# Seven-product gate and up projections in the first FFN of a two-block transformer kernel

## The chip, the cores and the metric

One core of one Trainium2 chip runs the kernel. The metric is the device time of one execution in microseconds (us); the kernel before takes 1641.35 us (median of three runs, 1639.81 to 1642.16).

## What is computed

A sequence of 512 tokens with model width 1024 goes through two transformer blocks, in fp32. Only the first block's feed-forward network (FFN) changes:

```python
h = rms_norm(x, norm_ffn_g)
x = x + (silu(h @ w_gate_ffn) * (h @ w_up_ffn)) @ w_down_ffn   # 1024 -> 2816 -> 1024
```

The second block has an FFN of the same size (with a causal convolution), which stays as it is. Every matmul is done in three passes, high x high, high x low and low x high parts of weight and activation, in fp32r.

## The kernel before, in words

**Tiles and chunks.** Activations lie transposed: 8 blocks of 128 features by 512 tokens (`X`). Weights come as chunks of 128 x 1024 fp32 (512 KB, 8 tiles of 128 x 128). PLAN (L62 to L90) lists all 336 chunks in the order of use. SyncE (SP) loads chunk i into one of five `raw` buffers (`load`, L2813); before it issues, it waits until VectorE (DVE) has split chunk i-5 (L2819). ScalarE (ACT) copies `raw` to the high part `WH` (recorded at L1132), DVE subtracts to get the low part `WL` (L1828); there are three such pairs. TensorE (PE) then runs 24 matmuls on the chunk (8 tiles x 3 passes, `mm3`, recorded at L504). PE waits for the split chunk, so a late load stops everything.

**First FFN.** Hidden width 2816 is 22 tiles of 128. Gate and up projections take one chunk for each tile and each side, 44 in all, as 24 matmuls with 512 moving columns each. DVE scales by the rms factor, ACT applies silu, DVE multiplies. The down projection already uses Winograd's form of Strassen's seven products of 2x2 blocks for most of its work (`down`, L837): pairs of hidden tiles, pairs of output tiles and two halves of 256 tokens are the blocks. `combine` (L2128) and `pair_lo` (L2141) form the sums of activations in `TH` and `TL`; each product is a run of matmuls with 256 moving columns. Two phases hold 12 and 10 hidden tiles. In the second phase only half of the outputs are made with seven products; the rest is done plainly by `last` with 512 columns over the last 10 hidden tiles (LAST, L34).

**Sums of weights.** Seven products need sums of weight blocks too. They are made in HBM during the run. SP copies a plane (one quarter of a weight matrix, 2.88 MB) to `sums` in four pieces, each followed by one chunk load (`copy_in`, L2834). GpSimd (POOL) then issues one accumulating DMA, which adds a second plane to it (`sum_in`, L2693). The third and the fourth sums start from finished ones, so SP waits on a semaphore for POOL's DMA before it copies (L2836), and POOL for SP's copies (L2694).

**What sets the order.** Each engine has its own program. SP's is a plain list (L2845 to L2902): while it waits for something, it loads no chunk. In the mixer stage the order of POOL, PE, ACT and DVE is written out by hand (`mixer_order_pool` and its likes). POOL there masks attention scores (L2687) and adds the second branch's output to `X` (L2663, the last of eight additions ends at 353 us); behind it come `sum_in(1, 0, ...)` and `sum_in(1, 1, ...)`, the eight additions of the third branch, a wait for the reload of x, and `sum_in(1, 2, ...)`.

**The stretch 300 to 450 us.** Chunks 44 to 55 are `mix2`, 56 to 67 `mix0`, 68 to 75 `w_out`, then `wk_xa` and `wv_xa`, eight each. Before `w_out`, SP waits for POOL's last addition and then reloads memT (1 MB) and x (2 MB) with L2867 and L2869; `w_out` adds its result to the reloaded x, and each output's PSUM bank (of three) is held until that add is done.

## Time and profile before

| what | value |
|---|---|
| median of three runs | 1641.35 us |
| span of the profiled execution | 1636.7 us |
| PE busy | 1621.8 us, 99% |
| DVE busy | 1010.2 us, 62% |
| ACT busy | 731.6 us, 45% |
| DMA moved | 225.96 MB, mean 138 GB/s |

The profiled execution's own time is known as its span, 1636.7 us from its first to its last instruction; the runs' median is 4.65 us above that. A busy share of PE says how long matmuls were in flight; the pitch from one matmul's start to the next says how fast they go. "Landing" of a DMA is the time from issue to its last byte. The software queue is POOL's (the accumulating DMAs), the hardware queue SP's.

### The profile page before, as it was taken

Reading aid. Unit: us, or ns where it says so; the run is one execution under the profiler, and the core shown is the slowest. Engines: PE = TensorE matmul, PEld = TensorE weight load, DVE = VectorE, ACT = ScalarE, POOL = GpSimd, SP = SyncE. Lnnn points to the kernel's source line nnn. Section 1 sums busy time; section 2 is a strip of 40 time slices with the busy share of each in tenths; the row PEclk is TensorE's granted clock in tenths of the full one; section 3 lists DMA queues with packets and bytes.
Section 4 is the critical chain, followed back from the end, with each engine's and each line's share of the span. In section 5 each row is a group of like instructions: output and inputs, shape, how many; then the busy total and the mean of one; then the engine's idle time right before and its main releaser. Section 6 shows DMA issues by size and latency. Waiting matters only on the chain.

```text
span 1636.7 us, 21111 instructions
## 1 busy us (share of the span) xinstructions
PE 1621.8 (99%) x8434; PEld 1342.7 (82%) x8434; DVE 1010.2 (62%) x1460; ACT 731.6 (45%) x1105; POOL 153.5 (9%) x172
## 2 busy tenths in 40 slices
PE   9999999999999999999999999999999999999999
PEld 7788878888878778888988887877777888898889
DVE  5346754455663454656656576757655588867886
ACT  5344334333553344334433356256685554544453
POOL 0000001221210011000000051212201200000000
DMA  7343222348754115768776443332114232363226
GB/s 258 102 183 113 91 91 65 101 128 268 227 164 141 52 65 164 223 212 217 217 241 189 126 158 116 117 129 65 65 39 131 81 104 92 114 201 109 91 89 181
DMA packets 60083, 225.96 MB, mean 138 GB/s; under 512 B 6657, under 2 KB 7041, under 8 KB 56337
## 3 DMA queue, kind: packets, MB, share of 16 engines
q1 hardware_dynamic: 55856, 197.29, 36.0%
q0 software_dynamic: 3840, 26.77, 7.6%
q8 instruction: 67, 1.10, 0.3%
q10 hardware_dynamic: 288, 0.54, 0.1%
q14 instruction: 32, 0.25, 0.0%
HBM read 220.35 MB, written 50.36 MB: 165 GB/s over the span
## 4 chain that ended last, share of the span: by engine, by line
PE 94%; DVE 2%; ACT 2%; issue 1%; DMA 0%; POOL 0%; SPq 0%; DVEq 0%; ACTq 0%; POOLq 0%
PE pst L504 93%; PE pst L1013 1%; PE pst L672 1%; DVE WL L1828 1%; ACT WH L1132 0%; DMA raw<-wst 0%; ACT L1137 0%; DVE qx L2072 0%; ACT misc L1132 0%; POOL acc L2653 0%; DVE XL L1840 0%; PE pst L794 0%; DVE ML L1836 0%; DVE misc L2607 0%; DVE X L2178 0%
## 5 line engine op out<-in xcount | busy, mean ns | idle before, releaser
L504 PE MATMUL pst<-XH,WH 128*128 128x512 f32 x1312 | 523.0, 399 | 0.6 <-DVE WL L1828 0.6
L1828 DVE TENSOR_TENSOR WL<-raw,WH 128x1024 fp32r<-128x1024 f32 (+2 forms) x334 | 381.5, 1143 | 220.1 <-ACT WH L1132 219.4
L504 PE MATMUL pst<-XH,WL 128*128 128x512 f32 x1312 | 511.6, 390 | 0.0
L504 PE MATMUL pst<-XL,WH 128*128 128x512 f32 x1312 | 511.1, 390 | 0.0
L1132 ACT ACTIVATE WH<-raw 128x1024 fp32r<-128x1024 f32 (+3 forms) x336 | 326.4, 975 | 314.5 <-PE pst L504 308.3
L504 PEld LDWEIGHTS pst<-XH,WH 128*128 128x128 f32 x1312 | 246.3, 188 | 61.4 <-issue 11.5
L504 PEld LDWEIGHTS pst<-XL,WH 128*128 128x128 f32 x1312 | 246.5, 188 | 52.0 <-issue 2.6
L504 PEld LDWEIGHTS pst<-XH,WL 128*128 128x128 f32 x1312 | 246.3, 188 | 51.9
L504 PE MATMUL pst<-TH,WH 128*128 128x256 f32 (+1 forms) x586 | 170.6, 291 | 1.6 <-DVE X L2178 1.0
L504 PE MATMUL pst<-TL,WH 128*128 128x256 f32 (+1 forms) x586 | 170.2, 290 | 0.0
L504 PE MATMUL pst<-TH,WL 128*128 128x256 f32 (+1 forms) x586 | 170.1, 290 | 0.0
L1132 ACT ACTIVATE misc<-misc 128x512 f32<-128x512 f32 x86 | 54.3, 631 | 148.8 <-DVE misc L2239 80.7
L504 PEld LDWEIGHTS pst<-TH,WH 128*128 128x128 f32 x586 | 112.3, 192 | 4.2 <-issue 1.7
L504 PEld LDWEIGHTS pst<-TL,WH 128*128 128x128 f32 x586 | 112.3, 192 | 1.7
L504 PEld LDWEIGHTS pst<-TH,WL 128*128 128x128 f32 x586 | 112.3, 192 | 1.6
L504 PE MATMUL pst<-ZH,WH 128*128 128x512 f32 x224 | 89.2, 398 | 0.0
L504 PE MATMUL pst<-ZH,WL 128*128 128x512 f32 x224 | 87.3, 390 | 0.0
L504 PE MATMUL pst<-ZL,WH 128*128 128x512 f32 x224 | 87.3, 390 | 0.0
L2653 POOL TENSOR_TENSOR acc<-acc,misc 128x512 f32<-128x512 f32 x35 | 59.3, 1695 | 280.5 <-ACT misc L1132 279.2
L2607 DVE SCALAR_TENSOR_TENSOR misc<-gp,colsb,misc 128x512 f32<-128x512 f32 x88 | 66.1, 751 | 23.4 <-ACT misc L1132 21.8
L1132 ACT ACTIVATE TH<-misc 128x512 fp32r<-128x512 f32 (+1 forms) x88 | 50.8, 586 | 45.0 <-DVE misc L2614 31.6
L1132 ACT ACTIVATE misc<-gp,colsb 128x512 f32<-128x512 f32 x44 | 35.9, 815 | 58.2 <-DVE gp L2633 58.2
(286 smaller groups left out, 1905.0 us busy)
## 6 DMA issues: line engine op xcount, KB each, us to landing
raw<-wst SPq DMA_DIRECT2D x237, 512.0 KB, 3.4
sums<-wd POOLq DMA_DIRECT2D x8, 2816.0 KB, 19.8
raw<-sums SPq DMA_DIRECT2D x32, 384.0 KB, 3.2
sums<-wd SPq DMA_DIRECT2D x16, 704.0 KB, 5.8
sums<-sums SPq DMA_DIRECT2D x16, 704.0 KB, 6.0
raw<-wd SPq DMA_DIRECT2D x24, 384.0 KB, 3.1
raw<-sums SPq DMA_DIRECT2D x24, 320.0 KB, 3.0
raw<-wd SPq DMA_DIRECT2D x18, 320.0 KB, 3.1
```

The costliest lines, as they stand in the source:

```text
L504: return nc.tensor.matmul(out, lhs, rhs, start=start, stop=stop, skip_group_check=more)
L672: ins = nc.tensor.transpose(ps[b0 + e][:, j * P:(j + 1) * P], sg_[:, s, e, j * P:(j + 1) * P], ident)
L1013: ins = nc.tensor.transpose(ps[b0 + e][:, j * P:(j + 1) * P], Sx[:, s, e, j * P:(j + 1) * P], ident)
L1132: return nc.scalar.activation(out, in_, func, **kw)
L1828: vec.tensor_tensor(WL[:, i % NHL, 0:n], raw[:, i % NRAW, 0:n], WH[:, i % NHL, 0:n].bitcast(F32), ALU.subtract).then_inc(wl, 1)
L2607: vec.scalar_tensor_tensor(o, gp[:, e, j:T + j], col[:, a:a + 1], o, ALU.mult, ALU.add).then_inc(hs, 1)
L2653: gp.tensor_tensor(acc[:, which, :], acc[:, which, :], sq[j % 2], ALU.add).then_inc(acp, 1)
```

## The change

1. The gate and up projections become seven products for each hidden tile: the 2x2 blocks are (even, odd input tiles) x (gate, up) for weights and (even, odd input tiles) x (token halves) for activations. Each product is 4 x 3 matmuls of 256 columns. 154 products go in pairs into 77 chunks of 1024, in a hand-made order (`up_order`).
2. Partial results are carried in PSUM: ACT copies product p1 into the bank where p2 accumulates, and p6 into the bank where p5 and p3 follow; two SBUF copies go to `acc`. In the second and third phase a matmul on `ones_r` primes the banks of the first two tiles.
3. The sums of the normed input are made once by `gained` (ACT and DVE), during `wo_xa`.
4. The hidden tiles go in three phases of 8, 8 and 6. The down projection's chunks hold two products. `last` covers 6 hidden tiles.
5. Sums of the gate and up weights are new (plane 5.77 MB; 8 copy pieces and 2 accumulating DMAs each); all copies and sums get new places in SP's and POOL's programs.

The diff, cut to its core:

```diff
-LAST = 10
+LAST = 6
-PAIRS = ((0, 6), (6, 5))
+PAIRS = {1: ((0, 4), (4, 4), (8, 3)), 2: ((0, 6), (6, 5))}
+DOWN_SEQ = {1: (MP_SEQ, MP_SEQ, MP_SEQ[:14]), 2: (MP_SEQ, MP_SEQ)}
+UP_N = HID * 4 * P * P
+PIECES = (2, 1, 1)
+def up_order(ph):
+    a, z = TILES[1][ph][0], TILES[1][ph][-1]
...
+    for m in range(a + 2, z + 1):
+        order += [(m, "p6"), (m - 1, "p3"), (m, "p7"), (m, "p2"), (m, "p5")]
+        order += [(m + 1, "p1")] if m < z else []
+        order += [(m - 1, "p4")]
+    return order + [(z, "p3"), (z, "p4")]
...
+            def ups1(ph):                                  (PE)
+                first = TILES[1][ph][0]
+                for x, (m, prod) in enumerate(UP_SEQ[ph]):
+                    if x % 2 == 0:
+                        h, l = (units(w) for w in chunk("ffn_up1"))
...
+                    if prod == "p1":
+                        if ph and m < first + 2:
+                            free(m % 2)
+                            mm(ps[m % 2][:, :], ones_r[:, :], XCH[:, 0:T]).then_inc(u_prime.sem, 1)
+                        free(4 + m % 2)
...
+                    elif prod in ("p2", "p6"):
+                        pe.wait_ge(u_seed, m + 1)
+                        if prod == "p2" and UP_AT[m, "p6"] < UP_AT[m, "p2"]:
+                            pe.wait_ge(u_seed2, m + 1)
...
+                    for k in range(4):
...
+                        ins = mm3(up_bank(m, prod), h[:, w, :], l[:, w, :], XCH[:, t], XCL[:, t], not more and k == 0, k == 3, more)
...
+                    if prod == "p1":                       (ACT)
...
+                        run(ACT.Copy, up_bank(m, "p2"), up_bank(m, "p1")).then_inc(u_seed.sem, 1)
+                    elif prod == "p6":
+                        run(ACT.Copy, up_bank(m, "p5"), up_bank(m, "p6")).then_inc(u_seed2.sem, 1)
...
+                        run(ACT.Copy, acc[:, m % 2, 0:256], up_bank(m, "p6")).then_inc(u_s.sem, 1)
+                    elif prod == "p5":
+                        run(ACT.Copy, acc[:, m % 2, 256:T], up_bank(m, "p5")).then_inc(u_y.sem, 1)
...
+                def half_b(m):                             (DVE)
...
+                    vec.tensor_tensor(U, up_bank(m, "p7"), U, ALU.subtract).then_inc(u_b.sem, 1)
+                def half_a(m):
...
+                    vec.tensor_tensor(U, up_bank(m, "p4"), U, ALU.subtract).then_inc(u_a.sem, 1)
...
+            def sum_in(w, to, plane, ready):               (POOL)
+                rows_ = [a.rearrange("(r c) -> r c", c=2048) for a in (sums[w][to], parts[w][plane])]
+                pool.wait_ge(d_copy if w else xs_out, ready)
+                for x in range(PIECES[w]):
+                    gp.dma_start(rows_[0][352 * x:352 * x + 352], rows_[1][352 * x:352 * x + 352], accum_op=ALU.add, max_dma_last_dim=8192).then_inc(d_sum if w else eg_in, 16)
...
+                    if x == 22:
+                        sum_in(0, 0, 3, 256)
+                        sum_in(0, 1, 3, 256)
...
             follow(mixer_order_pool, {"main": twice(mixer()), ...
+            sum_in(0, 2, 0, 384)
             sum_in(1, 0, 3, 128)
             sum_in(1, 1, 3, 128)
             drain(branch(2))
+            sum_in(0, 3, 1, 512)
             pool.wait_ge(x_in[3], 32)
+            for k in range(7):
+                add_squares()
             sum_in(1, 2, 0, 192)
+            sum_in(1, 3, 1, 256)
...
+            def copy_in(w, to, src, ready=None, pace=1):   (SP)
+                if ready:
+                    sp.wait_ge(d_sum if w else eg_in, ready)
...
+                for x in range(4 * PIECES[w]):
+                    nc.sync.dma_start(rows_[0][176 * x:176 * x + 176], rows_[1][176 * x:176 * x + 176]).then_inc(d_copy if w else xs_out, 16)
+                    load(pace)
...
-            load_to("zu", 0, 5)
-            copy_in(1, 0, wd[0][2])
-            copy_in(1, 1, wd[0][0])
-            load_to("mix0", 9, 5)
-            copy_in(1, 2, sums[0][0], 32)
+            load_to("q", 2, 5)
+            copy_in(0, 0, wup[2])
+            copy_in(0, 1, wup[0])
+            load_to("mix1", 5, 5)
+            copy_in(0, 2, sums[0][0], 64)
+            copy_in(1, 0, wd1[2])
+            copy_in(1, 1, wd1[0])
+            copy_in(0, 3, sums[0][2], 96)
             load_to("w_out", 0, 6)
             sp.wait_ge(mm_, DONE["mix0", "branch", 7])
...
-            load_to("ffn_up1", 1, 5)
-            copy_in(1, 3, sums[0][2], 48)
...
+            copy_in(1, 2, sums[1][0], 32)
+            load_to("wq_xa", 2, 5)
+            copy_in(1, 3, sums[1][2], 48)
+            load_to("ffn_up1", len(UP_SEQ[0] + UP_SEQ[1]) // 2, 5)
+            copy_in(2, 0, wd2[2], pace=3)
+            copy_in(2, 1, wd2[0], pace=3)
```

The words in brackets at the right name the engine whose program the lines belong to. The sums for the second FFN's down projection move to later places as well.

## Rows read from the trace of the kernel before

**Rows 1.** The page: span, and busy time of PE.
```profile
span 1636.7 us, 21111 instructions
PE 1621.8 (99%) x8434; PEld 1342.7 (82%) x8434; DVE 1010.2 (62%) x1460; ACT 731.6 (45%) x1105; POOL 153.5 (9%) x172
```

**Rows 2.** The chain that ended last, by engine.
```profile
PE 94%; DVE 2%; ACT 2%; issue 1%; DMA 0%; POOL 0%; SPq 0%; DVEq 0%; ACTq 0%; POOLq 0%
```

**Rows 3.** Windows: stretch, its length, then busy us of PE, PEld, DVE, ACT, POOL.
```profile
640.00:758.00 118.00, 117.75 (x519) 97.17 (x519) 70.33 (x101) 42.05 (x58) 2.80 (x3) 1.00 0.76 216
```

**Rows 4.** Timeline of PE in the gate and up projections: start, us, 512 columns.
```profile
699.75 0.39 PE L504 MATMUL pst<-XH,WH 128*128 128x512 f32 x1
...
705.87 0.39 PE L504 MATMUL pst<-XH,WH 128*128 128x512 f32 x1
```

**Rows 5.** Timeline of PE in the down projection, 256 columns.
```profile
799.73 0.28 PE L504 MATMUL pst<-TH,WH 128*128 128x256 f32 x1
...
802.61 0.28 PE L504 MATMUL pst<-TH,WH 128*128 128x256 f32 x1
```

**Rows 6.** Lines by form, 640 to 758 (WL) and 758 to 814 us (the others).
```profile
L1828 DVE TENSOR_TENSOR WL<-raw,WH 128x1024 fp32r<-128x1024 f32 x21 | 25.7, 1222 | 18.6 <-ACT WH L1132 18.6
L2178 DVE TENSOR_TENSOR X<-X,pst 128x256 f32<-128x256 f32 x13 | 5.5, 420 | 4.0 <-PE pst L504 3.6
L1132 ACT ACTIVATE ev<-pst 128x256 f32<-128x256 f32 x8 | 3.1, 384 | 7.9 <-PE pst L504 7.9
```

**Rows 7.** SP's loads at L2822 up to 322 us: chunks 1 to 57.
```profile
L2822 SPq DMA_DIRECT2D raw<-wst x57: 327/328/817, 3.1 to 321.4; - x57
DMA to landing us min/median/max: 3.2/3.4/11.5
```

**Rows 8.** Timeline of POOL in the mixer, and its DMAs at L2696.
```profile
153.71 0.40 POOL L2687 TENSOR_SCALAR_AFFINE_SELECT sg<-sg 128x256 f32<-128x256 f32 x1
...
351.80 1.68 POOL L2663 TENSOR_TENSOR X<-X,misc 128x512 f32<-128x512 f32 x1 [1.10 <-DVE misc L1915]
353.42 2.14 POOL L2696 DMA_DIRECT2D sums<-wd  x2
...
417.10 1.80 POOL L2663 TENSOR_TENSOR X<-X,misc 128x512 f32<-128x512 f32 x1 [0.68 <-DVE misc L1915]
431.55 0.92 POOL L2696 DMA_DIRECT2D sums<-wd  x1 [12.65 <-DMA X<-xT]
```

**Rows 9.** Timeline of PE: the first matmul of chunk 58.
```profile
361.74 0.39 PE L504 MATMUL pst<-ZH,WH 128*128 128x512 f32 x1
```

**Rows 10.** DMA queues from 355.5 to 359.5 us: packets, MB, share of 16 engines.
```profile
q0 software_dynamic: 90, 0.74, 92.8%
```

**Rows 11.** DMA queues and SP's loads (count, KB, landing) from 360 to 388 us.
```profile
q0 software_dynamic: 604, 4.82, 82.6%
q1 hardware_dynamic: 600, 2.20, 21.0%
...
raw<-wst SPq DMA_DIRECT2D x5, 512.0 KB, 14.9
```

**Rows 12.** POOL's eight accumulating DMAs, issue to landing; SP's wait for them.
```profile
DMA to landing us min/median/max: 18.6/19.8/36.1
SPq L2839 <- DMA sums<-wd: 2.1, 1, 2.1
```

**Rows 13.** SP's loads from 388 to 392 us, when POOL's DMAs had ended.
```profile
raw<-wst SPq DMA_DIRECT2D x2, 512.0 KB, 5.6
```

**Rows 14.** Timeline of SP: the reload of memT and x.
```profile
420.74 0.33 SPq L2867 DMA_DIRECT2D qx<-memT  x1
421.11 2.81 SPq L2869 DMA_DIRECT2D X<-xT  x4
```

**Rows 15.** DMA queues from 424 to 431.5 us, that reload.
```profile
q1 hardware_dynamic: 1280, 2.97, 102.5%
```

**Rows 16.** Timeline of PE at the kernel's start: matmuls of 512 columns.
```profile
1.52 5.49 PE L504 MATMUL pst<-ZL 128*128 128x512 f32 x12 [1.52 <-DVE ZL L1850]
```

More of the change, by code:

```diff
@@ L114, in main_counts @@
                     tile[name, 4 + m] = n
+        elif name in DOUBLE:
+            for x in range(2):
+                n += 1
+                tile[name, 2 * i + x] = n
         elif name == "w_out2" and i == 3:
@@ L198, in wait_ge, with program @@
             self.engine.wait_ge(sem, value)
-def program(nc, xT, memT, wst, wd1, wd2, cols, rows, wsp, cmat, cmask, outT):
+def program(nc, xT, memT, wst, wup, wd1, wd2, cols, rows, wsp, cmat, cmask, outT):
     es = ExitStack()
@@ L231, in program @@
         cd = nc.dram_tensor("cd", [16, T], F32, kind="Internal").ap()
-        wd = [wd1, wd2]
-        sums = [nc.dram_tensor(f"sums{n}", [4, PLANE_N], F32, kind="Internal").ap() for n in (1, 2)]
+        parts = [wup, wd1, wd2]
+        sums = [nc.dram_tensor(f"sums{n}", [4, UP_N if n == 0 else PLANE_N], F32, kind="Internal").ap() for n in range(3)]
         sty = ExitStack()
@@ L436, in program @@
         for w in range(2):
-            for ph in range(2):
-                for mp in range(2 if w == 0 and ph else 4):
+            for ph, seq in enumerate(DOWN_SEQ[w + 1]):
+                for mp in range(len(seq) // 7):
                     g = w, ph, mp
@@ L837, in product @@
                     if ks[0] == 0:
-                        got[mp, prod] = [units(w) for w in chunk(f"ffn_down{which}")]
+                        x = n * (len(got) % 2) if which == 1 else 0
+                        if x == 0:
+                            pair[:] = [units(w) for w in chunk(f"ffn_down{which}")]
+                        got[mp, prod] = [w[:, x:x + n, :] for w in pair]
                         if prod == "p2":
@@ L887, in ffn @@
             def ffn(which):
-                for ph in range(2):
-                    ups(which, TILES[ph])
+                for ph, tiles in enumerate(TILES[which]):
+                    if which == 1:
+                        ups1(ph)
+                    else:
+                        ups2(tiles)
                     down(which, ph)
@@ L2145, in pair_lo @@
                 if m % 2 == 0:
-                    w = T if which == 1 and m >= 12 else 256
+                    w = T if wide(which, m) else 256
                     t = slice(place(which, m), place(which, m) + w)
@@ L2636, in ups2 @@
                 combine(2, ms[-1])
-            for ph in range(2):
-                ups2(TILES[ph])
+            for ph, tiles in enumerate(TILES[2]):
+                ups2(tiles)
                 down(2, ph, lambda n: None)
@@ L2885, in sp_program @@
             nc.sync.dma_start(xs.rearrange("k p t -> p k t"), X[:, :, :]).then_inc(xs_out, 16)
+            load_to("aqk0", 2, 5)
+            copy_in(2, 2, sums[2][0], 96)
             load_to("w_out2", 0, 6)
@@ L2893, in sp_program @@
             nc.sync.dma_start(X[:, 0:4, :], xs[0:4].rearrange("k p t -> p k t")).then_inc(xb_in, 16)
+            load_to("ffn_up2", 8, 5)
+            copy_in(2, 3, sums[2][2], 112)
             load(NCH)
```

459 lines of the change are left out of this document (304 added, 155 removed).

## The prediction, made before the changed kernel was run

> **What bounds the kernel now.** The page first [rows 1]: of 1636.7 us PE has matmuls in flight for 1621.8. The chain of waits [rows 2] says the same from the other side: 94% of what set the end is PE. So time changes by how long PE's matmuls take, and by every wait that makes PE stand. The windows [rows 3] show the projections: in 118 us PE is busy for 117.75, DVE for 70.33. The timelines give the pitch. At 512 columns 27 matmuls lie between 699.75 and 705.87 [rows 4]: 0.2267 us each. At 256 columns 24 lie between 799.73 and 802.61 [rows 5]: 0.120 us, more than half of 0.2267. The rest of the reading is about DMA, since SP's list is also the list of loads.
>
> **Parts that make matmuls fewer.** Gate and up: 44 chunks x 24 = 1056 matmuls x 0.2267 = 239.4 us become 22 tiles x 7 products x 4 x 3 = 1848 x 0.120 = 221.8, so -17.6. Down: before, 28 x 6 x 3 + 14 x 5 x 3 = 714 narrow matmuls and 4 x 10 x 3 = 120 wide; after, 336 + 336 + 126 = 798 and 72. That is +10.1 - 10.9 = -0.8. Four primers add 0.9. Sum: **-17.5 us**. TensorE: Matmul & The Clock Gate in the Trainium skill (Back-to-back issue gap) has N/2.4 ns plus 2.5 for a warm matmul; as an estimate from that page the projections' part would be 26 us rather than 17.6. The trace's pitches disagree with it at both widths, and the trace decides.
>
> **Work beside PE in the FFN.** A hidden tile now takes 84 x 0.120 = 10.08 us of PE. Before it took 48 x 0.2267 = 10.88, in which DVE was busy for 70.33/118 x 10.88 = 6.48 [rows 3]. Added to DVE: 1.5 chunk splits of 1.22 and two 256-column reads of PSUM of 0.42 [rows 6]: 9.15, or 91%. ACT gets 1.5 chunk copies and four 256-column copies at 0.38 [rows 6], which fit. DVE is hidden with nine tenths of the cover used up. A wait of PE's own stands at the head of phases 2 and 3: p2 follows p6 at once and waits for a copy of 0.38, some 0.7 us each time. At a phase's end the last tile's combine, copy and split are covered by 8 us of products, in the last phase by 6. I take +3 us for all this, ends 0 and 12 (half a microsecond a tile).
>
> **The order of loads.** This is the largest part. After `load_to("mix1", 5, 5)` SP has issued chunks up to 41. Eight pieces of `copy_in(0, 2)` bring chunks 42 to 49, four each of `copy_in(1, 0)` and `copy_in(1, 1)` bring 50 to 57. Then SP waits for `eg_in` 96, that is for both accumulating DMAs of `sum_in(0, 2)`. Chunk 57 went out at 321.4 us [rows 7]. But POOL has `sum_in(0, 2)` behind its hand-made mixer order, whose last addition starts at 351.80; the DMAs in that place were issued at 353.42 [rows 8]. Behind SP's wait is every load from chunk 58 on, and PE needs 58 at 361.74 [rows 9].
>
> When does the wait end? POOL's queue alone moves a packet of 8 KB in 0.928 x 4 x 16 / 90 = 0.66 us of one of 16 engines [rows 10]. The sum's 5.77 MB are 736 of them: 30.4 us, first packet 2 us after the issue, so the wait ends near 386. In the run before, with loads beside it, a pair in this place took 36.1 us, to 389.5, and SP waited 2.1 us for it [rows 12].
>
> What comes after the wait is slow too. `sum_in(1, 0)` and `sum_in(1, 1)`, another 736 packets, follow on POOL's queue at once. Rows 11 show what such a pair does to the hardware queue: 604 packets of one, 600 of the other, one by one, 0.61 and 0.16 us long, and the loads got 2.20 MB in 28 us, 79 GB/s, landing after 14.9 us instead of 3.4 [rows 7, 11]. A copy piece (88 packets of 8 KB; at the 2.97 MB in 7.5 us of [rows 15] one takes 0.33 us) and a load (128 packets of 4 KB) then need (88 x 0.94 + 128 x 0.77)/16 = 11.4 us. Chunk 58 lands at 386 + 2 + 11.4 = 399.4; ACT's copy and DVE's split take 2.3, and PE starts it near 402, 59 near 413, 60 near 424.5. After 3.4 such pairs POOL's packets are out and loads keep up. Chunk 60 would have begun at 361.74 + 2 x 5.44 = 372.6. **Cost 52 us.** Lower end: POOL's second pair does not hinder, the load lands 5.6 us after the issue [rows 13], cost 386 + 5.6 + 2.3 - 361.7 = 32. Upper end: the wait ends at 389.5, cost 56.
>
> **The reload of x.** `sum_in(0, 3)`, two more DMAs, now stands before POOL's wait for the reload of x, not behind it. POOL reaches it when its last addition ends, 417.10 + 1.80; SP sends memT and x at 420.7 to 423.9 [rows 8, 14]. Without rival those ran at 1280 packets in 7.5 us [rows 15]. Packet for packet against 0.61 us ones, each round is 0.61 + 0.10, so 736 rounds take 33 us and carry 736 of about 1360; the rest is out at about 459 instead of 431. The PSUM banks of `w_out` wait for the adds to x, and chunk 74 is behind x in SP's queue: a copy piece and it land at 462, split at 464, where PE would have begun it at 361.74 + 16 x 5.44 = 449. **Cost 14 us**, ends 0 (the small packets are served in larger groups) and 18.
>
> The other waits have slack. `sum_in(0, 0)` and `(0, 1)` can start at 154 [rows 8] and take four DMAs, twice 36.1 us; SP asks for them some 16 chunks before 57, near 220, and a load has 35 us from issue to use (57 went out at 321.4 and PE began it at 361.74 - 5.44). The later sums of `wd1` and `wd2` end tens of microseconds before their use.
>
> **Clock.** The granted clock is 1.00 [rows 3], but there is no stand of PE beyond 3 us in this trace. The first twelve matmuls took 5.49 us [rows 16], 0.44 each instead of 0.2267: 2.6 us for one cold start at 1.2 GHz. Before chunks 58, 60 and 74 PE would stand; a slow 58 is hidden in the wait for 59. I add **3 us**, ends 0 and 5. The same page of the Trainium skill (Why this matters for your kernels) warns of such gaps; no row of this run shows one.
>
> **Sum.** 1636.7 - 17.5 + 3 + 52 + 14 + 3 = 1691.2 for the span; the median lies 4.65 above the profiled span, so 1696 us. All lower ends give 1636.7 - 17.5 + 32 + 4.65 = 1656, all upper ones 1715.
>
> **Rivals.**
> 1. *SP's wait starves PE only until the first sum lands.* The queues share better than rows 11 say, and x arrives in time. For it: bytes, not packets, might be what is shared. Against it: 14.9 us for landings in rows 11. All lower ends: 1656; with 3 us of FFN waits and 3 of clock 1662. Chance 0.14.
> 2. *Faster.* One mechanism: `sum_in(0, 2)` is done before PE runs dry, so loads go on. Then only the matmuls count: 1641.35 - 17.5 + 3 = 1627 (with x late as well 1641). It decides at 360 us: by then `eg_in` must be 96. For it: SP's and POOL's counts might be reached otherwise than I read, and POOL's queue is idle until 353. Against it: POOL's eighth addition needs chunk 55, and PE finishes that at 361.74 - 2 x 5.44 = 350.9. Chance 0.11.
> 3. *DVE becomes the bound of the projections.* Each tile's chain of copies, splits and subtractions, in order on DVE, takes 11 instead of 9.15 us: 22 x 0.9 = 20 us more, 1716 on top of the forecast. For it: 91% load and waits that interleave with ACT. Against it: splits are made two chunks ahead, 5.8 us. Chance 0.05.
> 4. *No change.* The stalls and the savings cancel: a single short stall of about 15 us. Chance 0.02.
>
> The forecast itself has 0.68. The range 1655 to 1710 holds it and rival 1. A measurement of this kernel tells 0.2%, 3 us, from nothing. Faster by more: 0.11; within: 0.02; slower: 0.87.
>
> **What would show it.** Step by step: pitches of 0.227 and 0.120 in the new trace and no more than 4 us of PE idle in the first FFN. SP's wait on POOL's DMA before `copy_in(0, 3)` of about 60 us, PE idle before chunk 58 of about 40 us and shorter stands before 59 and 60, with WL as releaser. Loads landing after 10 us or more there. x landing 30 us after its issue. If SP's wait is short, the prediction is wrong by its main term; if it is long and PE's idle time is 25 us or so, the sharing of the queues was misjudged.

## The result, and the profile after

The changed kernel takes 1726.28 us (median of 4 runs, 1723.07 to 1727.10) where the kernel before takes 1641.01 (median of 4, 1639.81 to 1642.16): the ratio is 1.0517, interval 1.0505 to 1.0530. It is slower by 85 us, where 55 were forecast, and the time lies above the range.

In the new trace PE's matmuls are recorded at L564, the weight remainders WL at L1989, ACT's copies at L1234, SP's loads at L3060 and L3075, its copies and their wait at L3082, POOL's accumulating DMAs at L2891 and its additions of squares at L2885. The page first, as in [rows 1]: span and busy times.

```profile
span 1721.3 us, 23389 instructions
PE 1625.6 (94%) x9266; PEld 1380.2 (80%) x9266; DVE 1086.5 (63%) x1584; ACT 805.2 (47%) x1241; POOL 157.9 (9%) x180
```

PE was busy for 99% and is for 94%. Its busy time grew by 4 us although matmuls were saved: part of them ran slowly. Next, which waits PE and SP have (line, what it waited for, us in total, times, longest).

```profile
PE pst L564 <- DVE WL L1989: 58.3, 7, 38.2
PE pst L564 <- DVE TL L1997: 12.3, 6, 3.4
PE pst L564 <- ACT pst L1234: 4.3, 3, 3.4
```
```profile
SPq L3082 <- DMA sums<-wup: 67.9, 2, 61.7
```

To see where the time goes, take the start of the same matmul in both traces and subtract. This gives the ledger of the case; everything below refers to it. It is made of one trace of each kernel.

| stretch | delay at its end | cost | predicted |
|---|---|---|---|
| up to chunk 57 | -0.3 | 0 | 0 |
| chunks 58 to 70 (SP's wait) | 48.5 | 48.8 | 52 |
| chunks 71 to 76 (reload of x) | 66.7 | 18.2 | 14 |
| rest of `wk_xa` to `wo_xa` | 73.5 | 6.8 (5.3 + 1.5) | 0 |
| first FFN | 80.0 | +6.5 | -17.5 + 3 |
| end of the FFN to the cf products | 84.1 | 4.1 | 0 |
| rest of the kernel | 84.7 | 0.6 | 0 |
| slow clock | inside the lines above | some 14 | 3 |

**SP's wait.** The timeline of SP: chunk 57's load goes out, and the next DMA is the copy behind the wait.

```profile
321.02 0.33 SPq L3060 DMA_DIRECT2D raw<-wst  x1
383.04 0.48 SPq L3082 DMA_DIRECT2D sums<-sums  x1
```

POOL comes to `sum_in(0, 2)` when its last hand-placed addition is done, and sends the next two sums directly behind it, as at 353.42 in [rows 8]:

```profile
351.46 1.67 POOL L2901 TENSOR_TENSOR X<-X,misc 128x512 f32<-128x512 f32 x1 [1.10 <-DVE misc L2076]
353.07 1.93 POOL L2891 DMA_DIRECT2D sums<-wup  x2
354.28 2.65 POOL L2891 DMA_DIRECT2D sums<-wd  x2
```

The wait ended at 383.0; 386 was forecast. What PE made of it (its timeline; in brackets the idle time before an instruction and what ended it):

```profile
361.17 0.39 PE L564 MATMUL pst<-XH,WL 128*128 128x512 f32 x1
399.71 0.79 PE L564 MATMUL pst<-ZH,WH 128*128 128x512 f32 x1 [38.16 <-DVE WL L1989]
...
495.33 0.77 PE L564 MATMUL pst<-ZH,WH 128*128 128x512 f32 x1 [14.13 <-DVE WL L1989]
```

Chunk 58 starts 38 us late, 59 and 60 another 4 each. In the DMA queues from 384 to 412 us, beside [rows 11], both queues have work all the time, and the loads land 29 us after their issue:

```profile
DMA packets 967, 7.60 MB, mean 272 GB/s; under 512 B 96, under 2 KB 96, under 8 KB 414
q0 software_dynamic: 521, 4.14, 71.4%
q1 hardware_dynamic: 446, 3.47, 31.3%
sums<-sums SPq DMA_DIRECT2D x7, 704.0 KB, 30.5
raw<-wst SPq DMA_DIRECT2D x7, 512.0 KB, 29.2
```

Without the 96 that are under 512 B, 505 packets of 8 KB (0.63 us each) in POOL's queue stand against 318 of 4 KB (the loads, 0.17 us) and 48 of 44 KB (the copy pieces, 1.68 us). A piece of 704 KB is thus 16 packets, and not the 88 of 8 KB that the prediction counted. That the queues take turns packet by packet is also what the Trainium skill states in DMA: Bandwidth & Descriptors (Queues, rings and completion order). By that rule the queue with the smaller packets gets fewer bytes. The trace agrees where packets are small, 436 packets of 3.44 MB against 434 of 1.55 MB in this window of the reload, 474 to 494 us; whether they alternate strictly isn't shown by counts:

```profile
q0 software_dynamic: 436, 3.44, 82.5%
q1 hardware_dynamic: 434, 1.55, 20.8%
```

**The reload.** SP sent x at 469.6 to 471.4; in the row of its DMAs (landing: least, median, most) it came 24 to 34 us later, since `sum_in(0, 3)` had been issued at 467.3.

```profile
L3115 SPq DMA_DIRECT2D X<-xT x4: 472/552/592, 469.6 to 471.4; - x4
DMA to landing us min/median/max: 23.7/32.8/34.0
```

PE then stands before chunk 71 (the row at 495.33 above), whose load had landed at 450.2. DVE's timeline says why: its first addition to the reloaded x waits for x, and the split of chunk 71 comes behind it in DVE's program.

```profile
493.36 0.69 DVE L2213 TENSOR_TENSOR X<-X,pst 128x512 f32<-128x512 f32 x1 [23.08 <-DMA X<-xT]
493.96 1.22 DVE L1989 TENSOR_TENSOR WL<-raw,WH 128x1024 fp32r<-128x1024 f32 x1
```

**The rest of `wk_xa`.** Its 6.8 us are two stands. The first, 3.52 us at 536.77, and slow matmuls behind it cost 5.3; POOL's next transfer was issued at 535.24, when PE already stood (from 533.2), so that it isn't the cause. DVE and ACT are late there with the chunk, behind `w_out`'s last output and the keys of the memory. The second, 1.09 us at 557.63, costs 1.5: ACT had waited 5.78 us for a load beside that transfer.

**The FFN.** The windows (length, busy time and count of PE, PEld, DVE, ACT and POOL, then PE's granted clock, DMA share, GB/s):

```profile
361.20:399.70 38.50, 0.35 (x2) 0.00 (x0) 1.27 (x2) 1.06 (x1) 0.00 (x0) 0.55 1.03 238
399.70:420.00 20.30, 14.96 (x50) 11.56 (x51) 4.81 (x6) 3.26 (x4) 0.61 (x1) 0.84 1.03 273
...
788.00:795.00 7.00, 4.37 (x27) 4.17 (x27) 6.34 (x12) 2.86 (x6) 0.00 (x0) 0.77 0.54 182
795.00:917.00 122.00, 120.54 (x984) 119.69 (x984) 91.20 (x135) 65.97 (x100) 0.00 (x0) 0.99 0.53 170
...
840.00:918.00 78.00, 77.01 (x639) 76.71 (x639) 61.00 (x87) 47.16 (x77) 0.00 (x0) 1.00 0.55 180
...
917.00:925.00 8.00, 5.38 (x34) 5.17 (x33) 6.74 (x12) 3.21 (x6) 0.00 (x0) 0.79 0.55 174
```

Between the heads of the phases PE is full (120.54 of 122) and DVE has air: 75% over this window, which holds part of the down projection too, and 78% in the projections alone (840 to 918 us). In the two short windows around a stand DVE is at 91% and 84%. PE stands at the head of the FFN (the first row below) and at the start of each phase of the down projection:

```profile
706.58 0.55 PE L564 MATMUL pst<-XCH,WH 128*128 128x256 f32 x1 [3.40 <-ACT pst L1234]
...
792.41 0.58 PE L564 MATMUL pst<-TH,WH 128*128 128x256 f32 x1 [2.63 <-DVE TL L1997]
792.79 0.42 PE L564 MATMUL pst<-TL,WH 128*128 128x256 f32 x1
793.01 0.41 PE L564 MATMUL pst<-TH,WL 128*128 128x256 f32 x1
...
921.81 0.58 PE L564 MATMUL pst<-TH,WH 128*128 128x256 f32 x1 [2.62 <-DVE TL L1997]
```

The first two matmuls after the stand are 0.38 us apart, the next ones 0.21 instead of 0.120: 1.2 GHz for some 12 to 26 matmuls. Adding up what the pitches from 700.1 to 1061 us exceed 0.120 and 0.2267 by: four stands above 1.2 us cost 11.8, twelve of 0.5 to 1.2 cost 6.6, shorter ones 1.5, matmuls at the lower clock some 6, together 25.7. What is left is 335.1. The same subtraction takes 1.6 from the kernel before and leaves 352.8: 17.7 less, where 17.5 were forecast. So the matmuls did get cheaper as worked out, and the FFN gave it all back. By how much varies: with the same FFN program e1 to e4 take 356.4 to 362.9 us for it, the changed kernel 360.7, the kernel before 354.2.

**Behind the FFN.** POOL's timeline there:

```profile
1045.35 10.99 POOL L2885 TENSOR_TENSOR acc<-acc,misc 128x512 f32<-128x512 f32 x6 [338.54 <-ACT misc L1234]
1057.20 6.94 POOL L2885 TENSOR_TENSOR acc<-acc,misc 128x512 f32<-128x512 f32 x4 [0.86 <-ACT misc L1234]
1064.96 6.91 POOL L2885 TENSOR_TENSOR acc<-acc,misc 128x512 f32<-128x512 f32 x4 [0.83 <-ACT misc L1234]
```

These are the additions of squares for the next norms, 14 almost in a row. PE meanwhile goes from the FFN's end (1060.9) to the cf products (1066.85) in 5.9 us; before it took 1.8. A second stand follows 6 us later, where the matmuls with `ones_r` wait for DVE's `TL`: 3.44 us at 1073.31, 2.54 before. In the traces of e1 to e4, with the same program, the clock is low behind it, and from the FFN's end to the kernel's end they lose 7.2 to 8.0 us. Here it stayed at 1.00, and the ledger has 4.7.

### The profile page after: what moved, and what is told of

It is laid out like the page before. It is cut to its first block and busy times, and to the rows that moved or that the text cites. A ratio compares the mean times of both kernels' runs of the same rounds, so it can differ in the third digit from the quotient of the medians.

```text
span 1721.3 us, 23389 instructions
## 1 busy us (share of the span) xinstructions
PE 1625.6 (94%) x9266; PEld 1380.2 (80%) x9266; DVE 1086.5 (63%) x1584; ACT 805.2 (47%) x1241; POOL 157.9 (9%) x180
## 5 line engine op out<-in xcount | busy, mean ns | idle before, releaser
L1989 DVE TENSOR_TENSOR WL<-raw,WH 128x1024 fp32r<-128x1024 f32 (+2 forms) x358 | 422.1, 1180 | 301.7 <-ACT WH L1234 294.7
L1234 ACT ACTIVATE WH<-raw 128x1024 fp32r<-128x1024 f32 (+3 forms) x360 | 361.0, 1005 | 326.5 <-PE pst L564 243.3
L564 PE MATMUL pst<-XH,WH 128*128 128x512 f32 x960 | 387.2, 403 | 5.7 <-DVE misc L2070 2.8
L564 PE MATMUL pst<-XH,WL 128*128 128x512 f32 x960 | 375.6, 391 | 0.0
L564 PE MATMUL pst<-XL,WH 128*128 128x512 f32 x960 | 375.2, 391 | 0.0
L564 PEld LDWEIGHTS pst<-XH,WH 128*128 128x128 f32 x960 | 181.1, 189 | 53.5 <-issue 10.9
L564 PEld LDWEIGHTS pst<-XH,WL 128*128 128x128 f32 x960 | 180.9, 188 | 38.7
L564 PEld LDWEIGHTS pst<-XL,WH 128*128 128x128 f32 x960 | 181.2, 189 | 38.3 <-issue 2.6
L564 PE MATMUL pst<-TH,WH 128*128 128x256 f32 (+1 forms) x598 | 174.9, 293 | 10.4 <-DVE TL L1997 8.0
L564 PE MATMUL pst<-XCH,WH 128*128 128x256 f32 x616 | 175.9, 285 | 5.7 <-ACT pst L1234 4.3
L564 PE MATMUL pst<-XCL,WH 128*128 128x256 f32 x616 | 175.0, 284 | 0.0
L564 PE MATMUL pst<-XCH,WL 128*128 128x256 f32 x616 | 174.9, 284 | 0.0
L564 PE MATMUL pst<-TL,WH 128*128 128x256 f32 (+1 forms) x598 | 173.5, 290 | 0.0
L564 PE MATMUL pst<-TH,WL 128*128 128x256 f32 (+1 forms) x598 | 173.4, 290 | 0.0
L564 PE MATMUL pst<-ZH,WH 128*128 128x512 f32 x224 | 90.7, 405 | 52.3 <-DVE WL L1989 52.3
L564 PEld LDWEIGHTS pst<-TH,WH 128*128 128x128 f32 x598 | 116.5, 195 | 13.6 <-DVE TL L1997 8.8
L564 PEld LDWEIGHTS pst<-XCH,WH 128*128 128x128 f32 x616 | 117.6, 191 | 7.2 <-issue 3.6
L564 PEld LDWEIGHTS pst<-XCL,WH 128*128 128x128 f32 x616 | 117.6, 191 | 0.3
L564 PEld LDWEIGHTS pst<-XCH,WL 128*128 128x128 f32 x616 | 117.6, 191 | 0.0
L564 PEld LDWEIGHTS pst<-TL,WH 128*128 128x128 f32 x598 | 116.6, 195 | 1.0
L564 PEld LDWEIGHTS pst<-TH,WL 128*128 128x128 f32 x598 | 116.4, 195 | 0.9
L2885 POOL TENSOR_TENSOR acc<-acc,misc 128x512 f32<-128x512 f32 x35 | 56.4, 1611 | 523.2 <-ACT misc L1234 485.2
```

Of the source, the lines that this page charges most:

```text
L564: return nc.tensor.matmul(out, lhs, rhs, start=start, stop=stop, skip_group_check=more)
L1234: return nc.scalar.activation(out, in_, func, **kw)
L1989: vec.tensor_tensor(WL[:, i % NHL, 0:n], raw[:, i % NRAW, 0:n], WH[:, i % NHL, 0:n].bitcast(F32), ALU.subtract).then_inc(wl, 1)
L2885: gp.tensor_tensor(acc[:, which, :], acc[:, which, :], sq[j % 2], ALU.add).then_inc(acp, 1)
```

## The experiments

Theory at the start: the ledger's first two lines are SP's wait and the reload, both caused by where POOL's accumulating DMAs stand; the later lines are smaller losses of their own. Rival: the FFN itself costs the time, and the stalls only move it. Each kernel below is the changed one with the edit shown (cut to its core) or told; delays are against the kernel before, at the same matmul. Three things vary from run to run with nothing changed in them: the stand at 468 us behind the reload (chunk 78) by 0 to 4 us, POOL's additions, and whether the clock falls behind a given stand, so single traces are read to 3 us, medians to 1 to 2.

**e1_x_first.** POOL waits for x before it sends the sum `(0, 3)`.
```diff
-            sum_in(0, 3, 1, 512)
             pool.wait_ge(x_in[3], 32)
+            sum_in(0, 3, 1, 512)
```


> The changed kernel with one line moved: POOL waits for the reload of x before it issues the two accumulating DMAs of sum_in(0, 3), as before the change, not after. In the changed kernel PE loses 18.2 us in w_out (chunks 71 to 74) and 6.8 us in wk_xa. If the reload's sharing of the DMA engines with POOL's packets is the cause, the reload takes 10 us instead of over 30 and the loss in w_out falls below 3 us. But the two DMAs then run beside wk_xa, whose chunks PE takes every 2.7 us (over 180 GB/s) where rows 11 gave loads 79 GB/s: I expect 5 to 15 us of that back there, 1708 to 1722 us in all. Rival: the loss in w_out is a consequence of the late start (clock, order) and not of this order; then it stays at 18 us and the time at 1726.

Measured: 1715.72 us, ratio 1.0447 (1.0429 to 1.0465), 10.6 less. The delay is 50.1 both at chunk 61 and at 76: the loss at the reload is gone altogether. But it is 66.6 from chunk 84 on: 16.5 us are lost beside `wk_xa`, where the sum now runs. The reload is the order of two lines, and moving a transfer by a few microseconds moves its price to the next loads.

**e2_pair_later.** The two sums for the down projection behind the third branch's additions.
```diff
-            sum_in(1, 0, 3, 128)
-            sum_in(1, 1, 3, 128)
             drain(branch(2))
+            sum_in(1, 0, 3, 128)
+            sum_in(1, 1, 3, 128)
```


> The changed kernel with sum_in(1, 0) and sum_in(1, 1), the pair of POOL's DMAs that follows sum_in(0, 2), moved behind the additions of the third branch. SP's wait stays and should end at the same 383 us. If packets of POOL's queue and of the hardware queue alternate, it is this pair that makes the loads after the wait slow: without it chunk 58 starts near 391 us instead of 399.7, and the stands before chunks 59 and 60 (3.2 and 2.9 us) vanish, so that by chunk 61 some 31 to 34 us are lost instead of 48.5. If the loads after the wait are slow for another reason (SP's own copies ahead of them), chunk 58 still starts after 396 us. The pair then collides with the reload of x, so the whole time says nothing; one look.

Measured: 1733.88 us, a single run. PE's stand before chunk 58 falls from 38.2 to 29.5, and chunks 59 to 68 are 31.0 late; in the changed kernel it is 48.5 from 61 on. So 17.5 us of the first stall are POOL's second pair of transfers beside the loads, and 31 the wait alone. The time got longer because the pair now stands in the way further on: SP has a second wait, and chunk 74 is 72.6 late.

```profile
SPq L3082 <- DMA sums<-wup: 66.8, 2, 61.5
SPq L3082 <- DMA sums<-wd: 30.8, 1, 30.8
```

**e3_no_sp_wait.** SP's copy takes a source that needs no wait. The kernel leaves out the right value of this sum, so its output is wrong; bytes and pieces are the same.
```diff
-            copy_in(0, 3, sums[0][2], 96)
+            copy_in(0, 3, wup[0])
```


> The changed kernel with SP's wait for eg_in 96 taken away: copy_in(0, 3) copies an input plane instead of the sum that POOL is making, with the same number of bytes and pieces, so the sixth of the seven kinds of weight sums is made of other values and the wait has no reason. If that wait is what starves PE (48.5 us lost by chunk 61 in the changed kernel), PE runs through chunks 58 to 67 with under 3 us idle and the time falls by 42 to 50 us, to 1676 to 1684. Rival: POOL's four DMAs from 353 us on starve the loads by their share of the DMA engines alone; then 15 us or more of the loss stay and the time is over 1695. Second rival: slack elsewhere hid part of the stall, then less than 35 us come back.

Measured: 1689.14 us, ratio 1.0294 (1.0274 to 1.0313), 37 less, where 42 to 50 were expected. No delay to the start of chunk 68 (-0.2): without the wait the whole first stall goes. But POOL's transfers then still fill the queue when x is reloaded, and that loss grows from 18 to 32 us:

```profile
462.26 0.77 PE L564 MATMUL pst<-ZH,WH 128*128 128x512 f32 x1 [28.10 <-DVE WL L1989]
```

The two losses are not independent. POOL's first four transfers, issued from 353 us on, landed at 429.4, when x had been sent at 422.5; in the changed kernel they had landed at 421.5, 48 us before x was sent. The stall had given POOL's queue time to drain.

**e4_late_plane.** The plane's copies and its sum move behind the reload.
```diff
-            copy_in(0, 3, sums[0][2], 96)
...
             load_to("wq_xa", 2, 5)
+            copy_in(0, 3, sums[0][2], 96, pace=0)
...
-            sum_in(0, 3, 1, 512)
             pool.wait_ge(x_in[3], 32)
...
             sum_in(1, 2, 0, 192)
+            sum_in(0, 3, 1, 512)
             sum_in(1, 3, 1, 256)
```


> The changed kernel with the fourth sum of the gate and up weights made 150 us later: SP's copy_in(0, 3) goes behind the loads of wq_xa (all eight pieces at once), POOL's sum_in(0, 3) behind sum_in(1, 2). Both waits go, and nothing is left out. If the order of loads was all that went wrong before the FFN, PE reaches the first FFN within 3 us of the kernel before, and only what the FFN itself and the stage behind it cost is left: 6.5 us and 5 us in the changed kernel's trace. Expect 1650 to 1658 us. If seven products are the gain that 17.5 us of fewer matmul columns promise, it would be 1627; if DVE at nine tenths makes the FFN slow beyond its waits at the phases' ends, over 1660.

Measured: 1657.67 us, ratio 1.0096 (1.0079 to 1.0114). 68.6 of the 85 us are gone with the FFN's program untouched (358.1 us in this trace, 360.7 in the changed kernel), which ends the rival. No delay through chunk 83; 6.8 from 84 on, where none to 3 were expected, after one stand while loads ran beside the transfer of `(1, 2)` (465.8 to 485.9 us):

```profile
488.11 0.80 PE L564 MATMUL pst<-WH,MH 128*128 128x512 f32 x1 [3.68 <-DVE WL L1989]
```

**e5_spread_sums.** e4 with the two remaining planes moved as well, `copy_in(1, 2)` behind `wq_xa`'s loads and `copy_in(1, 3)` with its sum into the FFN's first loads.

> The late-plane kernel, with the copies and DMAs for the third and fourth sum of the down weights spread too: copy_in(1, 2) behind the loads of wq_xa, copy_in(1, 3) in the first FFN, so that no accumulating DMA of POOL's runs beside wk_xa and wv_xa, whose chunks PE takes every 2.7 us. The late-plane kernel still loses 6.8 us there. If that is sum_in(1, 2)'s share of the DMA engines, the loss goes and the time falls from 1657.7 to 1650 to 1652 us. If it is the memory-key work of ACT and DVE, which has the same place in both, it stays at 1657.

Measured: 1658.13 us, ratio 1.0106 (1.0080 to 1.0132): a miss. The 6.8 us at chunk 84 are gone (2.4 lost at chunk 78 are the stand that comes and goes in all runs), but the last transfer now ran beside the FFN's loads (656.7 to 676.4 us), and PE stood there:

```profile
678.28 0.38 PE L564 MATMUL pst<-XCH,WH 128*128 128x256 f32 x1 [3.21 <-ACT pst L1234]
```

**e6a_phase_end.** e5, and in the projections DVE's combine of a phase's last tile but one comes before the chunk split, its remainder one product earlier.
```diff
+                    if was(x, 1, "p4") and m == z - 1:
+                        combine(1, m)
+                    if was(x, 2, "p4") and seq[x - 2][0] == z - 1:
+                        pair_lo(1, z - 1)
                     if x % 2 == 0:
                         chunk()
```


> The spread kernel, with DVE's order changed at the end of each of the three phases of the projections: the combine of the last tile but one before the chunk split, and its pair_lo one product earlier. Theory: PE stands 2.8 to 2.9 us at each phase's start of the down projection (10 or 5 matmuls in), because p1 already needs the last pair's first tile at its last k, and DVE has its pair_lo behind two chunk splits and the additions of three products; behind each stand some 12 to 26 matmuls run at half pace. Moving it by 2 to 2.5 us takes 6 to 9 us off with the clock: 1642 to 1645 us if the spread kernel has 1651. Rival: DVE is simply full there (91% worked out); then other work of DVE is late in its place and less than 3 us come back.

Measured: 1652.61 us, ratio 1.0072 (1.0049 to 1.0095), 5.5 less than e5. The stands of 2.8 to 2.9 us (start to start) at the phase starts are gone; 1.3 and 1.7 us remain in the last phase. No work was taken from DVE: its order was the matter.

**e6_phase_seeds.** e6a, and ACT copies the first two tiles' p1 at the end of `gained`; the first phase runs p1 of tile 1 between p6 and p2 of tile 0.

> The phase-end kernel and two more edits of waits in the projections: ACT makes the first two seed copies before the last sums of the input, and in phases 2 and 3 product p1 of the second tile goes between p6 and p2 of the first. Theory: PE stands 3.7 us 24 matmuls into the projections, with 15 matmuls at half pace behind it, because ACT has a copy of 0.85, a square and a chunk copy ahead of the first seed; and 0.7 us at each of two phase heads. Expect 4 to 6 us less than the phase-end kernel: 1637 to 1640 us. If PE's stand there moves on to the next thing that ACT has late (the second half of the input's sums for p7), under 2 us.

Measured: 1647.75 us (10 runs), ratio 1.0042 (1.0026 to 1.0058), 4.9 less; in the traces 4.0 of it in the FFN. What is left in the FFN is mainly the stand of e5, and the DMA queues of 656 to 668 us show its cause, POOL's transfer ahead of the loads of 256 KB, which land after 14 us instead of 2.9:

```profile
q0 software_dynamic: 279, 2.29, 92.1%
q1 hardware_dynamic: 222, 0.42, 10.7%
...
raw<-wup SPq DMA_DIRECT2D x4, 256.0 KB, 14.8
```

**e7_narrow_adds.** e5 with POOL's last 14 additions 8 columns wide. The kernel leaves out the other 504 columns, so the norms behind are wrong.
```diff
-                add_squares(0)
-                add_squares(1)
+                add_squares(0, 8)
+                add_squares(1, 8)
```


> The spread kernel, in which POOL's last 14 additions of squares of the first FFN's output (for the two norms behind it) take 8 columns of 512; the norms behind are thus wrong. Theory: the stage behind the FFN is 5 us longer than before the change because POOL's 14 additions of 1.85 us in a row, 26 us, now begin only 16 us before PE's last product (27 us before the change, with LAST 10), and ACT's squares and DVE's last adds wait for them. Then 4 to 7 us come off: 1644 to 1647 if the spread kernel has 1651. Rival: ACT and DVE themselves are the bound there, with their copies, squares and splits; then under 2 us.

Measured: 1653.17 us, ratio 1.0075 (1.0047 to 1.0102), 5.0 less than e5; from the FFN's end to the cf products 1.8 us again. The chain of additions is the fourth loss.

**e8_dve_adds.** e6, with the second set of seven additions on DVE, each behind the next block's XL.
```diff
                 x_lo(m, gg[:, m:m + 1], 24 + n + 1)
+                if n >= 2:
+                    add_square(n - 1)
```


> The kernel of e6_phase_seeds, in which the second set of seven adds of squares behind the first FFN (which=1) goes to DVE, each one block later than its square; POOL keeps the first set. Theory: behind the FFN the norms wait for POOL's chain of 14 adds in a row (10.99, 6.94 and 6.91 us long in the changed kernel); with two engines it is about half as long and e7_narrow_adds, which cut it in another way, gained 5.0 us. Expected 1642 to 1645 us, 3 to 6 us below e6_phase_seeds' 1647.75; the stand of TensorE behind the last part of the FFN (3.8 us) falls under 2 us, and nothing else moves. Rival: DVE has no room in the last part of the FFN (six blocks of matmuls for each pair), so that its weight remainders come late instead: 1647 us or more, with new waits PE <- DVE WL in the last part.

Measured: 1645.79 us, ratio 1.0043 (1.0029 to 1.0056): 3 to 6 us less than e6 were expected. The time is 2.0 less, but the kernel before, run beside each, was 0.7 faster too, and e6's ratio is 1.0042: no difference is shown. The FFN ended 2.1 us earlier in the trace, but the stage behind it took 7.5 us (5.9 in e6). That POOL and DVE wait for one another there is the reading of e12's expectation, which e12 bears out.

**e9_early_sums.** e8, and all three late planes between the reload and `wo_xa`, their 12 copies in one burst.

> The kernel of e8_dve_adds, in which all three late sum planes (0,3), (1,2), (1,3) are copied and added between the reload of X and the loads of wo_xa, none of them beside the FFN's own loads. Theory: what stands of TensorE in the first FFN's projections (4.9 and 1.5 us in e6_phase_seeds, at 668 and 633 us) is the last POOL transfer beside the FFN's 183 GB/s of loads; where wk, wv and wo only want their ordinary rate it is hidden. Expected 4 to 7 us below e8_dve_adds: 1636 to 1641 us, ratio to the kernel before 0.997 to 1.000. Rival: three transfers in a row slow the loads of wk and wv as in e4_late_plane, where two did (6.8 us): then TensorE stands 7 us or more between 484 and 620 us and the time is 1643 to 1650 us.

Measured: 1646.40 us, ratio 1.0041 (1.0028 to 1.0053): the rival. The stand at 668 us is gone and the FFN 5.3 us shorter than before, but 9.0 us were lost at 550, where weight loads stood behind twelve copies in one queue and beside POOL's transfer of 523 to 556 us, and landed 39 us after their issue:

```profile
556.05 1.22 PE L564 MATMUL pst<-kx,qx 128*128 128x256 f32 x2 [6.00 <-ACT misc L1234]
```

**e10_all_dve.** e6 with all 14 additions on DVE, in front of the next block.

> The kernel of e6_phase_seeds with all 14 adds of squares behind the first FFN on DVE, those of a block done when DVE comes to the next one. In e8_dve_adds each engine waited for the other's add (blocks 2.8 us apart where ACT and PE needed less), and the stage between the FFN and the cf products still took 7.5 us where the kernel before needs 1.8. Theory: 14 DVE adds of 0.68 us fit beside DVE's other work there, so that this stage falls to 2 to 3 us: 1640 to 1642.5 us, ratio to the kernel before 0.999 to 1.002. Rival: what is late there is ACT's and DVE's own chain for each block (addition, XH, squares, XL), not the adds' engine: then 1645 us or more, as e8_dve_adds.

Measured: 1651.81 us, ratio 1.0071 (1.0058 to 1.0084): a miss. The stage took 11.4 us, 1.9 of them before its first matmul (the expectations below leave these out and say 9.4). DVE's row shows the new chain, two additions of 0.68 us in each block beside XL and the addition into X, with no idle time between:

```profile
995.57 0.68 DVE L2415 TENSOR_TENSOR X<-X,pst 128x512 f32<-128x512 f32 x1
996.16 1.48 DVE L2424 TENSOR_TENSOR acc<-acc,misc 128x512 f32<-128x512 f32 x2
997.56 0.75 DVE L2005 SCALAR_TENSOR_TENSOR XL<-X,colsb,XH 128x512 fp32r<-128x512 f32 x1
998.23 1.48 DVE L2424 TENSOR_TENSOR acc<-acc,misc 128x512 f32<-128x512 f32 x2
```

**e11_early_all.** e10 with the planes in the order (1,2), (0,3), (1,3), and weight loads between the bursts of copies.
```diff
             load_to("wq_xa", 2, 5)
+            copy_in(1, 2, sums[1][0], 32, pace=0)
+            load_to("wq_xa", 4, 5)
+            copy_in(0, 3, sums[0][2], 96, pace=0)
+            load_to("wo_xa", 0, 5)
+            copy_in(1, 3, sums[1][2], 48, pace=0)
```


> The kernel of e10_all_dve with the three late sum planes in another order and place: (1,2) first, then (0,3), then (1,3), copies in bursts with weight loads between them, all POOL transfers between 515 and 590 us and none beside the FFN's loads. In e9_early_sums, where twelve copies stood ahead of the weight loads in one queue, TensorE lost 9.0 us at 550 us and 2.5 at 465, but the FFN got 5.3 us shorter. Theory: both losses came from loads queued behind the burst of copies; with the burst cut up they go and the FFN's gain stays: 1635 to 1639 us, ratio 0.996 to 0.999, faster than the kernel before. Rival: the losses come with the POOL transfers themselves, three in 75 us beside wk, wv and wo: then 1641 to 1647 us with a stand of 4 us or more between 484 and 620 us.

Measured: 1643.42 us (10 runs), ratio 1.0022 (1.0013 to 1.0031), 8.4 less than e10 but above what was expected. It is the rival's time without the rival's stand. Of the theory the part on the burst held: from 484 to 620 us the delay doesn't grow (4.2 at both), the 9.0 us are gone, and so is the stand at 668. The order of the planes moved as well, so the burst alone isn't shown. The stand at 468 took 4.2 in this trace, and the stage behind the FFN 11.4.

What was open then was that last stage, and three kernels settled it.

**e12_split_chain, e14_pool_chain, e13_split_only.** e11's placement with POOL adding which=0 and DVE which=1 *before* it waits for the next block; the same placement with POOL alone; the changed kernel with only that split.
```diff
                 m = FINAL_ORDER[0][n]
+                if n >= 2:
+                    add_square(n - 1)
                 dve.wait_ge(*final(1, m))
```


> The kernel of e11_early_all with the adds of squares split between two engines in another way: POOL adds which=0, DVE adds which=1, and DVE does so before it waits for the next block of X, not behind its XL. Theory: in e8_dve_adds the DVE add of a block stood behind the next block's wait and XL and held ACT's squares, and in e10_all_dve DVE itself was the bound; with the add ahead of the wait neither holds, ACT needs 2.0 us for a block, and the stage from the end of the FFN to the cf products falls from 9.4 us to under 4.5: 1636.5 to 1640 us, ratio 0.998 to 1.0005. Rival: the blocks' chain PE, DVE's addition into X, ACT's XH and squares is the bound whatever engine adds: 1642 us or more.

> The kernel of e11_early_all with the adds of squares back on POOL alone, as in the change. Theory: POOL's chain costs 5.9 us between the end of the FFN and the cf products (e6_phase_seeds) against 9.4 with all adds on DVE, so 2 to 4 us less than e11_early_all: 1639.5 to 1642 us, and 2 to 4 us more than e12_split_chain. Rival: no difference to e11_early_all (1643.4), if the tail is bound by something that the three forms have in common.

> The changed kernel with nothing but the split of the adds of squares of e12_split_chain. Theory: the 5 us that the changed kernel lost between the FFN and the cf products (5.9 us where the kernel before had 1.8, and a later end of the last block) are POOL's chain of 14 adds, which the shorter last part (6 blocks of K for each tile in place of 10) no longer covers: 1720 to 1723 us, 3 to 6 us below the changed kernel's 1726.3. Rival: no change, 1725 to 1728 us.

| kernel | us (runs) | ratio, interval | FFN's end to cf |
|---|---|---|---|
| e12 | 1638.19 (11) | 0.9982, 0.9973 to 0.9992 | 4.7 |
| e14 | 1642.95 (11) | 1.0012, 1.0003 to 1.0021 | 6.8 |
| e13 | 1722.34 (4) | 1.0496, 1.0482 to 1.0510 | 4.7 |

e12 and e13 came as the theory had them, and the stage itself just above its 4.5 us. e13 takes 3.9 us off the changed kernel; by the ratios it is 3.4, and their intervals overlap slightly. e14 lies 1 us above its band and no further from e11 than the spread of their runs, so POOL alone against DVE alone is not told apart; either against the split is. POOL's timeline in e12 shows that now one addition stands in each block and DVE's releases the next:

```profile
971.34 1.67 POOL L2902 TENSOR_TENSOR acc<-acc,misc 128x512 f32<-128x512 f32 x1 [1.02 <-DVE acc L2423]
973.95 1.68 POOL L2902 TENSOR_TENSOR acc<-acc,misc 128x512 f32<-128x512 f32 x1 [0.94 <-DVE acc L2423]
```

e12 is also the one kernel that beats the one before, by 0.18% with the interval just clear of none. Its windows, the FFN and the stage behind it, then those of the kernel before:

```profile
626.80:975.90 349.10, 339.64 (x2725) 332.94 (x2724) 276.66 (x414) 202.56 (x314) 10.13 (x7) 1.00 0.58 188
975.90:980.60 4.70, 3.54 (x17) 0.67 (x16) 3.80 (x6) 2.84 (x5) 1.39 (x1) 1.00 0.69 210
```
```profile
626.40:981.00 354.60, 353.85 (x1898) 306.86 (x1897) 217.21 (x306) 139.21 (x195) 26.28 (x18) 1.00 0.66 195
981.00:982.80 1.80, 1.80 (x17) 0.43 (x16) 0.85 (x2) 0.99 (x2) 0.25 (x1) 1.00 0.40 105
```

Of the 17.7 us of matmuls saved, some 5.4 arrive at the FFN's end; 2.9 go again behind it. The rest is in PE's waits between products, up to 1.7 us each (339.64 busy of 349.10), which no run here took away. In this trace 3.3 us of the gain are left at 1063 us and 0.6 at the end: 1.7 went at 1228, where the clock fell behind a stand of 1.9 us that the kernel before has too and passes at full clock.

## Why the prediction was right or wrong

- **Right: sign and main mechanism.** SP's wait for POOL, and POOL's place behind the hand-made order, were named, with 62 us of wait (60 forecast), resumed at 383 (386), PE standing 38 us (40). e3 removes it and the delay is nothing through chunk 68. The term of 52 measured 48.8, and e2 (a single run) fits its two parts, 31 for the wait alone (32 was the lower end) and 17.5 for the second pair. The agreement is partly luck: 48.8 holds some 4 us of slow clock, which had a term of its own, so the waits made about 45. The wait ended 3 us early, and a copy piece with a load landed every 9.3 to 9.7 us where 11.4 were worked out, which fits that a piece is 16 large packets and gives POOL's queue fewer turns than 88. Rivals 1, 2 and 4 fell with it.
- **Right in kind, low by 4, by another path: the reload.** 18.2 us, forecast 14 with an upper end of 18 (its own 464 less 449 give 15); x took 24 to 34 us to land (30). e1 shows it to be the order of two lines on POOL. But the prediction had x delay PE through chunk 74, behind x in SP's queue. What stood was chunk 71, long landed, whose split waited behind DVE's addition to x. That no load was late is read from the trace; no run changed DVE's order there.
- **Right: fewer matmuls.** 17.7 us against 17.5.
- **Wrong, the step that failed: "I take +3 us for all this, ends 0 and 12".** The waits of PE in the FFN and their slow matmuls cost 25.7 us in the changed kernel and 1.6 in the kernel before, so +24 where the upper end was 12. The prediction summed DVE's work for an average tile and found 91%; in the projections' window DVE is at 78%. What stands in the way is the order at the ends. The prediction had the last tile's work "covered by 8 us of products"; what came late is the remainder of the last tile but one of each phase, which DVE's program had behind two chunk splits. And the first seed waits behind ACT's other copies, at the head of phase 1, where the prediction had no wait; the short waits that it had at the heads of phases 2 and 3 came as said (0.62 us each at 840.5 and 968.6, 0.7 forecast). e6a and e6 took 5.5 and 4.9 us off by order alone, with no work removed. Some 12 us of such waits are left in e12, and what they come from stays open. Rival 3 had the right place and, by luck, the size (20 us), and the wrong cause: no engine's mean load was the bound.
- **Missing: 6.8 us beside `wk_xa`.** The sentence on the later sums looks at when sums are used, not at what their transfers do to the loads next to them, though rows 11 had just been used for exactly that. In the changed kernel this cost 1.5 of the 6.8; in e1 it was 16.5, in e4 6.8, in e5 it moved into the FFN. The other 5.3 came before the transfer, at a stand that costs 0 to 4 us in e4 to e14, where nothing was changed in it.
- **Missing: 4.1 us behind the FFN.** The prediction counted the matmuls of LAST = 6 but not what the ten wide blocks had covered: POOL's 14 additions of 1.3 to 2.3 us. e7 gained 5.0 us with them narrow, e13 3.9 with them split.
- **Low: the clock.** 3 us with an upper end of 5, for three cold starts. Counted in pitches: some 4 in the first stall, 1.3 in the reload, 2.7 beside `wk_xa`, 6 in the FFN, some 14; most stands that the list above lacks brought their own.

The sum of the ledger: 30 us above the forecast are 21.0 in the FFN (6.5 against -14.5), 6.8, 4.2 and 4.1 more in the three places above and 0.6 at the end, less 3.2 of SP's wait and the 3 that stood for the clock. With the FFN's waits as forecast the time would have been 1705 us, inside the range.

## What to carry to other kernels

An accumulating DMA of several megabytes has a price wherever loads share its engines: before moving one, list every load issued in the 20 to 40 us after it, and keep waits for it out of the queue that feeds the matmuls. When matmuls get fewer or narrower, list what they covered at both ends of each stage, instruction by instruction in each engine's order; an average load of 78% says nothing about a phase's last tile. Where two engines share a chain of small steps, put each step before its engine's next long wait.

## What the runs showed of the hardware that was not expected

- The length of a stand did not decide whether PE came back at 1.2 GHz. In the changed kernel it did after 2.49 us of idle time at 419.36 (pitch 0.43 at 512 columns) and after 2.63 and 2.62 at 792 and 922 (pitch 0.21 at 256), and it did not after 2.50 at 1029 nor after 3.44 at 1073 (pitch 0.23 at 512). The same stand of 2.62 at the start of the second down phase was followed by the low clock in the changed kernel and in e1, not in e2, e3 and e4. Behind a stand of 1.9 us (1228 to 1239 us) the clock fell in e8, e11 and e12, while the 13 other traces of changed kernels pass it at full clock, and in e6 it fell at 957 behind stands of 1.04 and 1.44 us. The Trainium skill's warning of gaps (TensorE: Matmul & The Clock Gate, Why this matters for your kernels) held here in kind, for stands that come from an order of copies as much as for those from late loads; the gap length that it names does not sort these cases.
- A stall can hide another: removing one of 48.5 us gained 37 (e3), since POOL's queue no longer drained in it.
- A POOL addition of 128 x 512 took 1.28 to 1.42 us in e8 and 1.29 to 2.25 us in the changed kernel behind the FFN; a DVE one took 0.68. The four longest (2.09 to 2.25) ran beside a chunk split of DVE's, but two others beside a split took 1.4 and 1.6, so what stretches them isn't shown.
- A plain copy of 704 KB within HBM is 16 packets of 44 KB here, 1.68 us each; an accumulating transfer's packets are 8 KB, 0.63 us each.
